# One core, a stack of mixers: squares added on GpSimd ahead of one product of ones, rounding put ahead of squares, and the rotary keys' product a unit later

## What is computed

```python
# SSD, at its end: y in 8 groups of 256 features
y = y.reshape(bsz, seq, D_INNER) * jax.nn.silu(z)
y = rmsnorm(y.reshape(bsz, seq, SSD_GROUPS, D_INNER // SSD_GROUPS), gnorm.reshape(SSD_GROUPS, -1))
h = h + y.reshape(bsz, seq, D_INNER) @ ssd_w_out
...
h = h + gla_mixer(rmsnorm(h, gla_norm), ...)      # o @ gla_w_out is added in four parts
x = rmsnorm(h, final_norm)                        # the first block's last norm
u = rms_norm(x, norm_mix_g)                       # the second block's first norm, straight behind it
proj = u @ w_in                                   # latents, rotary key, convolution inputs, gates
k_rope = apply_rope(k_rope_raw, cos, sin)
```

## Time and profile before

| | us |
|---|---|
| three runs, median (lowest, highest) | 1793.48 (1792.98, 1796.91) |
| the profiled execution, whole | 1795.42 |
| its span, from first to last instruction | 1793.7 |
| PE busy | 1693.6 (94%) |
| VectorE busy | 1125.9 (63%) |
| ScalarE busy | 841.1 (47%) |
| GpSimd busy | 368.6 (21%) |
| mean granted share of TensorE's full clock | 0.978 |

### The profile page before, as it was taken

How to read it: one execution, slowest core, us unless ns; L and a number is a source line. 1 busy time by engine, 2 the same in 40 slices (tenths; PEclk the granted TensorE clock), 3 DMA queues, 4 the chain that set the end, 5 groups by cost and what they waited for, 6 DMA issues and landing times.

```text
span 1793.7 us, 20988 instructions
## 1 busy us (share of the span) xinstructions
PE 1693.6 (94%) x7944; PEld 1361.2 (76%) x7944; DVE 1125.9 (63%) x1520; ACT 841.1 (47%) x1365; POOL 368.6 (21%) x299
## 2 busy tenths in 40 slices
PE   6889999999979999999988899999899999999998
PEld 5667777777757778787866678887688688888886
DVE  6668777788767475756566767777556553434343
ACT  5666565666624354435345335446354442323232
POOL 0254554455541000000006212221220200000001
PEclk9999999999989999999998999999999999999999
DMA  3634444344212222222222323222233333333332
GB/s 105 182 120 127 129 118 140 119 136 123 83 29 82 59 71 71 72 81 70 61 75 60 82 60 82 64 73 88 82 92 98 93 93 96 94 95 102 97 94 71
DMA packets 260106, 164.58 MB, mean 92 GB/s; under 512 B 26909, under 2 KB 249286, under 8 KB 258982
## 3 DMA queue, kind: packets, MB, share of 16 engines
q1 hardware_dynamic: 260006, 163.25, 31.6%
HBM read 160.86 MB, written 2.36 MB: 91 GB/s over the span
## 4 chain that ended last, share of the span: by engine, by line
PE 72%; DVE 14%; ACT 6%; issue 4%; POOL 2%; DMA 1%; SPq 0%; DVEq 0%; ACTq 0%; POOLq 0%
PE stream L79 20%; PE stream L81 20%; PE stream L80 20%; DVE weights_lo L147 2%; DVE ssd_x L987 2%; ACT weights_hi L137 1%; PE q L782 1%; PE q L1969 1%; PE q L1993 1%; PE q L79 1%; PE q L81 1%; PE q L80 1%; DVE ssd_m L1065 1%; PE q L809 1%; POOL h_sum_of_squares L220 1%
## 5 line engine op out<-in xcount | busy, mean ns | idle before, releaser
L79 PE MATMUL stream<-u_lo,weights_hi 128*128 128x512 f32 (+2 forms) x1312 | 533.7, 407 | 12.1 <-DVE u_lo L249 4.5
L81 PE MATMUL stream<-u_hi,weights_hi 128*128 128x512 f32 (+2 forms) x1312 | 516.2, 393 | 0.0
L80 PE MATMUL stream<-u_hi,weights_lo 128*128 128x512 f32 (+2 forms) x1312 | 516.0, 393 | 0.0
L147 DVE TENSOR_TENSOR weights_lo<-weights_raw,weights_hi 128x1024 fp32r<-128x1024 f32 (+4 forms) x269 | 329.4, 1226 | 274.6 <-ACT weights_hi L137 274.2
L137 ACT ACTIVATE weights_hi<-weights_raw 128x1024 fp32r<-128x1024 f32 (+4 forms) x269 | 268.8, 1001 | 462.8 <-PE stream L81 435.3
L79 PEld LDWEIGHTS stream<-u_lo,weights_hi 128*128 128x128 f32 (+2 forms) x1312 | 248.4, 189 | 78.2 <-issue 11.0
L80 PEld LDWEIGHTS stream<-u_hi,weights_lo 128*128 128x128 f32 (+2 forms) x1312 | 248.9, 190 | 54.9 <-issue 4.7
L81 PEld LDWEIGHTS stream<-u_hi,weights_hi 128*128 128x128 f32 (+2 forms) x1312 | 248.0, 189 | 55.6 <-issue 0.7
L217 POOL COPY h_sum_of_squares<-h_squares 128x512 f32<-128x512 f32 x5 | 3.3, 650 | 798.5 <-ACT h_squares L205 798.5
L79 PE MATMUL stream<-mlp_a_lo,weights_hi 128*128 128x512 f32 x256 | 100.2, 391 | 0.0
L81 PE MATMUL stream<-mlp_a_hi,weights_hi 128*128 128x512 f32 x256 | 99.7, 389 | 0.0
(11 more groups left out here) (460 smaller groups left out, 2884.5 us busy)
## 6 DMA issues: line engine op xcount, KB each, us to landing
weights_raw<-in_w_mlp_dram SPq DMA_DIRECT2D x64, 512.0 KB, 3.8
weights_raw<-in_ssd_w_in_dram SPq DMA_DIRECT2D x48, 512.0 KB, 4.1
weights_raw<-in_gla_w_in_dram SPq DMA_DIRECT2D x40, 512.0 KB, 3.8
ssd_cum_steps<-ssd_cum_rows SPq DMA_DIRECT2D x32, 512.0 KB, 5.0
weights_raw<-in_w_in_dram SPq DMA_DIRECT2D x29, 512.0 KB, 3.8
ssd_exp_cum<-ssd_cum_pairs SPq DMA_DIRECT2D x16, 512.0 KB, 7.7
weights_raw<-in_ssd_w_out_dram SPq DMA_DIRECT2D x16, 512.0 KB, 3.6
weights_raw<-in_gla_w_out_dram SPq DMA_DIRECT2D x13, 512.0 KB, 3.4
```

Source lines behind the costliest of these rows:

```text
L79: pe.matmul(out, lh, rl, start=first, stop=False, skip_group_check=skip)
L80: pe.matmul(out, ll, rh, start=False, stop=False, skip_group_check=skip)
L81: return pe.matmul(out, lh, rh, start=False, stop=last, skip_group_check=skip)
L147: dve.tensor_tensor(lo, raw_view(c, n), hi.bitcast(F32), ALU.subtract).then_inc(c.w_split, 1)
```

## The change

Three edits. In the SSD, for the first seven of the eight groups, GpSimd adds the second tile of squares to the first in slot 1, ahead of its decays of slot 2, and TensorE's product of ones takes that one tile; the eighth group stays as it was. At the end of GLA ScalarE rounds `u` of both tiles of a slot before it squares either. In the mix TensorE's product for the rotary keys comes behind unit 8 instead of unit 7, and the two copies of its result a step later.

```diff
@@ GpSimd, SSD @@
+                if k == 1 and 0 <= i - 2 < SG - 1:
+                    pool.wait_ge(s_sq, 3 * (i - 2) + 2)
+                    pool.tensor_tensor(squares[:, 0, :], squares[:, 0, :], squares[:, 1, :], ALU.add)\
+                        .then_inc(s_sq, 1)
@@ TensorE, SSD @@
-                    pe.wait_ge(s_sq, 2 * f + 2)
-                    for p in range(2):
-                        last = pe.matmul(q[4][:, :], c.ones[:, :], squares[:, p, :], start=p == 0, stop=p == 1)
+                    tiles = 1 if f < SG - 1 else 2
+                    pe.wait_ge(s_sq, 3 * f + (3 if tiles == 1 else 2))
+                    for p in range(tiles):
+                        last = pe.matmul(q[4][:, :], c.ones[:, :], squares[:, p, :], start=p == 0, stop=p == tiles - 1)
@@ ScalarE, end of GLA @@
                     for m in range(m0, m0 + tiles):
+                        scale_tile(c, act, nx, m, free_value(c, out_tile(GH - 1, m)))
+                    for m in range(m0, m0 + tiles):
                         final = free_value(c, out_tile(GH - 1, m))
-                        scale_tile(c, act, nx, m, final)
                         square_tile(c, act, m, final)
                         square_tile(c, act, m, final, gain)
@@ TensorE, mix @@
-                if k == 7:
+                if k == 8:
                     pe.wait_ge(s_tb, 13)
@@ ScalarE, mix @@
-                if k == 8:
+                if k == 9:
                     act.wait_ge(s_j, 1)
```

## The result

| | before | with the change |
|---|---|---|
| median of 12 runs each (lowest, highest), us | 1793.06 (1791.91, 1796.91) | 1796.34 (1793.9, 1799.03) |
| ratio, with its 95% interval | | 1.0016 [1.0009, 1.0024] |
| the profiled execution, whole, us | 1795.42 | 1793.9 |

The interval is 1.6 to 4.3 us slower. The forecast was 2.4 us faster.

A forecast was written before the change was run, and what follows sets the result against it. VectorE's progress, not TensorE, was taken to bound the SSD rounds. First edit -2.7, u rounding +0.3, rotary product 0 gave -2.4 us: 1791.1 us from a median of 1793.48, range 1787.0 to 1798.0.

The forecast's parts named there:

- What bounds the kernel: SSD rounds: how early VectorE gets through its list sets the stretch, not TensorE, which stands 0.8 us behind VectorE each round.
- The shorter product: TensorE's product of ones L809: one float32 matmul of 0.86 us fewer in seven groups, 6.0 us if all follows.
- What the addition pushes: GpSimd's sum of squares moves four later instructions by 0.8 us, colliding with VectorE; first edit's sum -2.7 us.
- The walk: Instruction-by-instruction retiming of VectorE and GpSimd for groups two to six, all behind L809 0.86 us earlier; gains 0.65 each.
- The rule on SBUF: A VectorE instruction with two SBUF inputs and a GpSimd one reading SBUF exclude each other; first to issue goes first.
- Gain at each of the five: 0.65: Groups two to six each gain 0.65 us, provided VectorE's last L147 still precedes GpSimd's L708.
- the turned order: Rival, chance 0.24: GpSimd's L708 goes 0.02 us ahead of VectorE's last L147, delaying it 1.13 us; total 1797.9 us.
- The rival's price: L708 ahead of L147: five groups lose 0.48 us each, first 1.13, seventh 0.57; +4.1, with the second edit +4.4.
- u before the squares: End of GLA, ScalarE's rounding first: the first square comes later, GpSimd partly absorbs it; +0.3 us, between 0 and 0.6.
- The rotary product: Mix, rotary keys' product behind unit 8: waits move to units 8 and 9; 0 us, range -0.7 to +1.7.
- the clock's rival: Mix: TensorE's slow-clock stretch may fall on unit 9, costing 1.7 us in some runs; 1792.8 us, chance 0.07.
- The cover-whole rival: SSD: none of the addition's collisions with VectorE counts; 5.7 us gained in all, 1787.8 us, chance 0.22.

## Why the prediction was wrong, step by step

- **What bounds the kernel: right.** VectorE's list from slot 3 on sets the round. TensorE arrives earlier and waits for it.
- **The shorter product, 0.86 each: right in size.** The product alone gave 5.35 of 6.0 us, and 0.89 a round.
- **What the addition pushes: right, and it held the clue.** The walk named each collision: the second L1055 behind L735 (3.22 for the pair), 0.2 us lost at the L147 of slot 3 (1.40), L708 and L1024 in the other order (1.28 and 2.31), all found. It gave -0.65 a round if the last L147 goes first; with that order forced it measured -0.46, with 0.2 us of new collision at L1065 of slot 4 that the forcing itself brings.
- **The rule on SBUF that I leaned on holds.** In the rows shown here an instruction of VectorE with two inputs in SBUF and one of GpSimd that meet don't run at once: one of them is longer by what is left of the other (L147 2.34, L1029 2.31). L987 stays at 3.1 us beside L731. The Trainium skill (SBUF — State Buffer, section Who interferes with whom) says so too, and adds that whoever issues first goes first; the trace agrees down to 0.03 us.
- **The step that failed: "Gain at each of the five: 0.65, if VectorE's last L147 still goes first".** The condition didn't hold. GpSimd's L708 went first in all six rounds, and a round lost 0.34 us instead of gaining 0.65. I gave the condition 0.42 and the turned order 0.24, as I took 0.02 us for too little to read. But the rival's own times had GpSimd ahead (210.38 against 210.40), and in the rows of before both starts repeat within 0.01 us from round to round, so they leaned to the turn. What the rival said of the trigger, "With everything 0.86 earlier L921 is done before GpSimd's L735 is", was no reason for it: the product alone shows that L921 moves along and nothing turns. What counts is the 0.2 us of the walk, by which L1065, and with it L147 and L735, come later against L921. Carried one row further, the walk says that L921 then stops holding L708, and that L708's own chain (3.50) stands ahead of L147 (3.53). So the mechanism of the rival was right, and its trigger was put down to the wrong cause.
- **The rival's price.** It said +0.48 in each of five rounds, +1.13 for the turn in the first group and +0.57 in the seventh; with the second edit 4.4 us, 1797.9. Five rounds measured +0.34 each, 1.7: the turn cost 0.80 (58.14 against 57.34) where I had 1.13, and what it is set against is 0.46, not 0.65. It costs less than the 1.12 us by which it delays L147, as the 0.3 us that TensorE waits behind the later L955 with the order given back are gone. The sixth turn lies in the seventh group's piece, which takes 53.35 us against 51.86: +1.5, where 1.13 + 0.57 stood. With the order given back it is 52.58, so 0.7 is the pushed decays (the addition alone has 52.57), near my 0.57, and 0.8 the turn. The piece ahead of the rounds, with the first group's product, I had at 0. It takes 55.8 to 56.0 us in the three profiles with the first edit whole and 55.1 to 56.7 in four without any of it, so its part isn't settled.
- **u before the squares: +0.3 (0 to 0.6) forecast, +1.0 by the traces.** "GpSimd is behind by then in most slots and takes this up" was wrong: GpSimd idles 1.3 us in its chain before, waiting for L205, and 1.4 us with the edit, so its later start counts whole. The wait for the join grew as said (3.0 to 5.1), and `u_lo`'s shrank by 0.4 only.
- **The rotary product: 0, right**, with both waits where they were said to be, and the clock's rival cost nothing in any of the four profiles with this edit.
- Sum by the traces: 1.7 + 1.5 + 1.0 + 0 = 4.2 us, and what the first group does; the runs say 3.3 and 5.0. The time lay in the given range, 1787.0 to 1798.0, on the side of the rival. The cover-whole rival is out for an addition on GpSimd, and true of one on VectorE.

## What to carry to other kernels

Where a walk through two engines' lists ends in a tie, go on with it: write down for both sides which releaser holds them, and ask of every small delay found on the way which of them it moves; here 0.2 us on one side was worth 0.8 us a round. Two edits that are each free may use up the same slack, so a cost of 0 in a run of one alone says nothing of both. And a short instruction on an engine with much idle time is best placed by whom it stands in front of: the two joins, moved behind what TensorE waits for, gave 7.8 us with no work removed.

## What was not expected of the hardware

- The order of two instructions that want SBUF within 0.03 us of each other is stable: GpSimd 0.03 ahead went first in every round of the three profiles that have this tie, VectorE 0.06 ahead went first in every round of the seven others in which no semaphore sets the order.
- An instruction held back by a semaphore from the other engine came 1.38 us later, where the same one held back only by the other's use of SBUF ended 1.12 later.
